# The first gate/up pair by seven products in three chunk pairs instead of two, and two input groups fetched two loads apart

## The reference

```python
    h = h + jnp.concatenate([oa, ob, oc, od], axis=-1) @ w_out[i]
    y = _rms(h, norm_ffn_g[i])
    h = h + (jax.nn.silu(y @ w_gate[i]) * (y @ w_up[i])) @ w_down[i]
    y = _rms(h, norm_ple_g[i])
```

## Time and profile before

| | |
|---|---|
| median of 3 runs (lowest to highest) | 1379.96 us (1379.74 to 1380.36) |
| the profiled execution: its time, its span | 1380.99 us, 1379.2 us |
| matmuls | 6175, busy 1371.7 us of the span |
| weight chunks split on VectorE, whole (L1391), from `w_raw` and from sums | 431 and 104 |
| DMA from HBM | 296.19 MB read, 27.31 MB written, 235 GB/s |

### The profile page before, as it was taken

One profiled execution on the slowest core, in us unless ns is written; L12 is line 12 of the kernel. 1 busy time (PEld: TensorE's weight loads), 2 busy tenths in 40 slices (PEclk: granted clock), 3 DMA queues, 4 the chain that ended last, 5 costly groups with the idle time before them and its releaser, 6 DMA issues.

```text
span 1379.2 us, 16905 instructions
## 1 busy us (share of the span) xinstructions
PE 1371.7 (99%) x6175; PEld 1123.2 (81%) x6175; DVE 1142.5 (83%) x1315; ACT 878.5 (64%) x1173; POOL 151.2 (11%) x127
## 2 busy tenths in 40 slices
PE   9999999999999999999999999999999999999998
PEld 7888888888888888788888888888888887777886
DVE  6589986688999988899999889976666769886897
ACT  7476755576777555677756576755566656675564
POOL 2000010011111000111100011100000144420000
PEclk9999999999999999999999999999999999999999
DMA  9766658887999788899987889999877878889675
GB/s 334 247 212 212 201 161 283 273 247 242 293 283 262 229 261 256 251 275 264 282 267 245 247 258 248 278 318 298 257 238 270 282 237 261 271 253 294 197 249 169
DMA packets 182859, 351.90 MB, mean 255 GB/s; under 512 B 13073, under 2 KB 37901, under 8 KB 182648
## 3 DMA queue, kind: packets, MB, share of 16 engines
q1 hardware_dynamic: 160408, 291.66, 64.4%
q0 software_dynamic: 9280, 33.97, 12.6%
q10 hardware_dynamic: 13088, 25.18, 6.1%
HBM read 296.19 MB, written 27.31 MB: 235 GB/s over the span
## 4 chain that ended last, share of the span: by engine, by line
PE 84%; DVE 2%; DMA 1%; issue 1%; ACT 0%; POOL 0%; ACTq 0%; DVEq 0%; POOLq 0%
PE acc L2340 13%; PE acc L2343 13%; PE acc L2342 13%; PE acc L2159 11%; PE acc L2161 11%; PE acc L2160 11%; PE sp L2340 2%; PE tp L2340 2%; PE tp L2343 2%; PE tp L2342 2%; PE sp L2343 2%; PE sp L2342 2%; DMA wide<-w_raw 1%; PE sp L2455 1%; PE tp L2471 1%; DVE w_lo L1391 1%
## 5 line engine op out<-in xcount | busy, mean ns | idle before, releaser
L963 ACT ACTIVATE w_hi<-w_raw 128x1024 fp32r<-128x1024 f32 x453 | 474.2, 1056 | 308.6 <-PE acc L2161 207.5
L1391 DVE TENSOR_TENSOR w_lo<-w_raw,w_hi 128x1024 fp32r<-128x1024 f32 x431 | 523.5, 1228 | 150.3 <-ACT w_hi L963 147.8
L2159 PE MATMUL acc<-w_lo,hh 128*128 128x512 f32 x528 | 207.7, 393 | 0.0
L2161 PE MATMUL acc<-w_hi,hl 128*128 128x512 f32 x528 | 205.6, 389 | 0.0
L2160 PE MATMUL acc<-w_hi,hh 128*128 128x512 f32 x528 | 205.6, 389 | 0.0
L2340 PE MATMUL acc<-w_lo,yh 128*128 128x512 f32 x452 | 176.0, 389 | 0.0
L2342 PE MATMUL acc<-w_hi,yh 128*128 128x512 f32 x452 | 175.9, 389 | 0.0
L2343 PE MATMUL acc<-w_hi,yl 128*128 128x512 f32 x452 | 175.8, 389 | 0.0
L963 ACT ACTIVATE w_hi<-wide 128x1024 fp32r<-128x1024 f32 x104 | 110.2, 1060 | 71.9 <-DVE wide L1405 35.7
L1391 DVE TENSOR_TENSOR w_lo<-wide,w_hi 128x1024 fp32r<-128x1024 f32 x104 | 126.8, 1223 | 13.7 <-ACT w_hi L963 13.4
L2159 PE MATMUL acc<-w_lo,yh 128*128 128x512 f32 x352 | 137.6, 391 | 0.3 <-DVE w_lo L1391 0.3
(11 more groups left out here) (332 smaller groups left out, 2179.4 us busy)
## 6 DMA issues: line engine op xcount, KB each, us to landing
w_raw<-in_w_gate SPq DMA_DIRECT2D x88, 512.0 KB, 5.8
w_raw<-in_w_up SPq DMA_DIRECT2D x88, 512.0 KB, 6.3
w_raw<-in_w_down SPq DMA_DIRECT2D x88, 512.0 KB, 6.3
w_raw<-in_w_in SPq DMA_DIRECT2D x64, 512.0 KB, 4.6
wide<-w_raw POOLq DMA_DIRECT2D x52, 512.0 KB, 6.0
w_raw<-in_swa_w_in ACTq DMA_DIRECT2D x48, 512.0 KB, 5.0
w_raw<-in_w_out SPq DMA_DIRECT2D x32, 512.0 KB, 5.9
w_raw<-in_w_ple_gate SPq DMA_DIRECT2D x32, 512.0 KB, 5.3
```

The lines of the kernel that those rows point to most:

```text
L963: act.activation(w_hi[:, v % SPL], src, ACT.Copy).then_inc(hi_ready, 1)
L1391: dve.tensor_tensor(w_lo[:, v % SPL], src, w_hi[:, v % SPL].bitcast(F32), ALU.subtract).then_inc(lo_ready, 1)
L2159: pe.matmul(dst, xh[:, f, tk], w_lo[:, v % SPL, k], start=(f == 0), stop=False)
L2161: last = pe.matmul(dst, xl[:, f, tk], w_hi[:, v % SPL, k], start=False, stop=(f == CK * end + CK - 1))
```

## The change

`FIRST_PLAN` gets a third pair of chunks by seven products (chunks 2 of gate and up), and a new order: it begins with the first two quads, and the plain chunk 3 of gate and up comes after the middle. It has 22 items instead of 20, from the same 16 loads. `FIRST_AT` moves the other work: the third input group is taken behind item 1 instead of 3, the residual addition behind item 2 instead of 1, turn and squares behind 3 instead of 2, the fourth group behind 14 instead of 10, `m1`, `mix`, `gate` and `silu` behind 18 to 21. In SyncE's queue the put of the third group stands behind load 1 and its fetch behind load 3 (both behind load 4 before), the put of the fourth behind load 7 and its fetch still behind load 9.

```diff
-FIRST_PLAN = plain(0, 2) + plain(1, 2) + plain(0, 3) + plain(1, 3) + quad("g", 0) + quad("g", 1) + quad("u", 0)
-FIRST_PLAN += plain(0, 4) + quad("t", 0) + quad("s", 0) + plain(1, 4) + quad("u", 1) + plain(0, 5) + quad("t", 1)
-FIRST_PLAN += quad("s", 1) + plain(0, 6, 7) + plain(1, 5, 6, 7)
-FIRST_AT = dict(pool_low=19, resid=1, turned=2, low2=3, request=3, low3=10, m1=13, mix=18, gate=19, silu=19,
-                copied={2: [0], 5: [1]}, summed={0: 6, 1: 11})
+FIRST_PLAN = quad("g", 0) + quad("g", 1) + quad("u", 0) + plain(0, 4) + plain(1, 4) + quad("t", 0) + quad("s", 0)
+FIRST_PLAN += quad("u", 1) + plain(0, 5) + quad("t", 1) + quad("s", 1) + plain(1, 5) + quad("g", 2) + quad("u", 2)
+FIRST_PLAN += plain(0, 3) + plain(1, 3) + quad("t", 2) + quad("s", 2) + plain(0, 6, 7) + plain(1, 6, 7)
+FIRST_AT = dict(pool_low=21, low2=1, resid=2, turned=3, request=4, low3=14, m1=18, mix=19, gate=20, silu=21,
+                copied={0: [0], 4: [1], 10: [2]}, summed={0: 4, 1: 7, 2: 14})
...
-                if i == 4:
-                    move(T_FFN + 2)
+                if i == 1:
+                    put(T_FFN + 2)
+                if i == 3:
+                    fetch(T_FFN + 2)
+                if i == 7:
+                    put(T_FFN + 3)
                 if i == 9:
-                    put(T_FFN + 3)
                     sp_.wait_ge(turned_lo, low_count(T_FFN + 2))
                     fetch(T_FFN + 3)
```

## The result

The changed kernel takes 1387.14 us (median of five runs, 1385.54 to 1389.36), the kernel before 1379.96 (1379.65 to 1380.36, five runs): a ratio of 1.0047, interval 1.0035 to 1.0058. It is slower, by about 6.5 us by the ratio. The forecast, 1384.0, had the sign and not the size: 4.0 us of 6.5. The median lies 0.5 above the end of the range, 1386.6; by the ratio the time is 1386.4, just inside it.

The account below looks back on a forecast made before the run. TensorE, busy 99% of the span, was taken to set the end, with the order of the queues in front of it deciding. Saving, front and end, -0.68 + 3.20 + 1.48 = +4.0 us, gave 1384.0 us, range 1381.6 to 1386.6.

Parts of the forecast that it names:

- The saving: TensorE in the first gate/up pair: 183 matmuls in place of 186 save 0.68 us.
- The front: First items of the block: TensorE waits for late w_lo at items 3, 4, t, s and 8, 3.20 us in all.
- The end of the block: Two plain items instead of three after the last gate item: the next block starts 0.82 us late.
- Inside the second pair: VectorE enters the second pair less far ahead, so TensorE waits 0.25 + 0.27 + 0.02 us more there.
- in the third: Third pair, where VectorE has no lead at one place: TensorE waits 0.12 us more.
- Puts, fetches, loads 8 and 9: SyncE's queue: the new order costs 0 to 1.1 us, the latter if loads 8 and 9 land late; taken as 0.
- The failed step: GpSimd's third add, issued near 309.2, takes about 5.8 us; sum due near 315.6, product wanted at 323: hidden, no cost.
- A: Rival: VectorE runs at least 2.1 us ahead before t, so only the 0.68 saving is left: 1379.3 us; 10%.
- B: Rival: VectorE is about 1 us further ahead at w_lo(4), half of the later waits is left: 1381.6 us; 8%.
- The highest-occupancy rule: Optimise the engine with the highest occupancy first, here TensorE; by it alone the change gives -0.68 us.
- C: Rival: the third input group lands 1.0 us late, or loads 8 and 9 cost 1.1, or both: 1385 to 1386.1; 15%.
- D: Rival: new gaps bring TensorE's clock from 2.4 to 1.2 GHz, 50 matmuls cost 11 us more: 1395; 2%.

Follow-up runs that it names:

- e9: e7 with ScalarE's third copy of tops ahead of item 12 instead of item 10; 1380.71 us, ratio 1.0002.
- e1: The changed kernel with the first sum of weights behind item 3 instead of item 4; 1387.69 us, ratio 1.0051.
- e3: The changed kernel with chunks 2 of gate and up as plain items, so two quads, 186 matmuls and no third add; 1384.95 us, ratio 1.0033.
- e8: e2 with a new end: three plain items behind the last gate item, gate chunk 6 ahead of the last sums; 1382.5 us, ratio 1.0015.
- e4: The kernel before with only SyncE's new order of puts and fetches; 1380.59 us, ratio 1.0002.
- e5: The changed kernel's new plan with SyncE's old order of puts and fetches; 1387.79 us, ratio 1.0056.
- e6: e2 with the first sum and the second copy of tops one item earlier; 1382.79 us, ratio 1.002.
- e7: The edits of e6 and e8 together, front and end; 1381.71 us, ratio 1.0009.
- e2: The changed kernel with loads 12 to 15 held until GpSimd's third add by DMA has landed; 1385.14 us, ratio 1.0035.

## Why the prediction was wrong in size

The sign, the places and the sizes of the waits at the front and at the end were right; one term, put at nothing, was not.

- **The saving.** 3 x 0.2267 = 0.68 us: right. The page has three matmuls fewer, and e9, in which the order costs next to nothing, comes out within 0.1% of the kernel before.
- **The front.** Forecast 0.14 + 0.69 + 0.35 + 1.59 + 0.43 = 3.20; measured 0.13, 0.58, 0.33, 1.57, 0.39 = 3.00, at the items named. Following three queues with the durations of the rows was good to 0.11 us in each term. That the chain from the first sum to t and s is its core is shown by e1 (the sum moved by one item, both waits gone), that the third quad has no part in it by e3.
- **The end of the block.** Forecast 0.82, measured 0.85; shown by e8, where one more item under the gate sum and silu removes it. Inside the second pair 0.34 instead of 0.54, in the third 0.11 instead of 0.12. Sum 1.30 for 1.48. In e8 the second pair's waits went with the end's, which bears out that they were its late start handed on.
- **Puts, fetches, loads 8 and 9.** Taken as 0 of a possible 1.1: right for the changed kernel (0.08 at the second quad's s), and e4 shows it for the queue by itself in the old plan. With the new plan the new queue does matter: e5, without it, waits at load 10. And the 0 held only for this front: with the front mended, load 9 is what ScalarE waits for, 3.96 us in e1, 2.19 in e6 and 3.10 in e7.
- **The failed step: "GpSimd's third add by DMA takes about 5.8 us [...] hidden".** The place (309.2) was right and the duration was not: 9.5 us instead of 5.8, and the sum that waits for it stalls VectorE's queue until 318.72, not 315.6. TensorE did not wait for the third quad's product, which the forecast had as its only reader, but for item 15, whose low part stands behind the sum in VectorE's order. It cost 1.74 us where 0 was given, and no bound was kept for it. The row that was used is a median over eight adds of 140 us; in the changed kernel's page the median of 53 adds is 6.2, while the one that mattered met five loads. e2 shows the cause: 6.1 us with three of the five held back. With 1.74 added, the forecast of 1384.0 becomes 1385.7; the ratio puts the kernel at 1.0047 x 1379.96 = 1386.4.
- **Sum.** By its own terms the profiled execution should have taken 1385.0 and took 1385.91: +1.74 for the add, -0.20 at the front, -0.18 at the end, +0.08 at the second quad give +1.44, and the stretch before the first pair was 0.45 shorter: 1386.0. The third pair starts at 379.63, forecast 379.0: the later pairs did not win the time back.
- **The rivals.** A (the saving stays) and B (half of it) would need VectorE 1 to 2 us earlier at item 4; its low part there ends at 298.39, 0.5 before the 298.91 of the forecast, and 0.45 of that is the earlier start of the whole stretch. Both are refuted. The highest-occupancy rule of the Trainium skill, "Perfetto Trace Analysis", section "Identifying the Most-Contended Engine", taken alone as the prediction took it, would have given 0.68 less; measured were 6.5 more. The same section does not take TensorE's matmul share as a measure of its headroom and looks at the share of its weight loads instead, which is 81% in the earlier trace rows, beside VectorE's 83%. C (transfers) had the right kind of event at two wrong transfers, and its 15% were too few for "some transfer of this block lands late", which happened in the profiled executions of five of the eight kernels with three quads (the changed one, e1, e5, e6, e7; in e1, e6 and e7 it is load 9, which C names). The range reached to 1386.6 only for the sake of C, whose two events cost 0.08 here. That the time by the ratio lies inside it is luck. D (the clock): not in the profiled run, but in e1 in full, at 2.8 us, a quarter of the 11 that it was priced at.

What stays open: the median of the changed kernel is 1.2 us above its profiled run. Its longest run (1389.36) has a mean clock of 0.999, and so have runs of e1; the two longest of e5 (1388.89 and 1390.0) have 0.998 and 0.999. That the wait of 1.74 grows in some executions until the clock falls, as in e1, would fit but was not traced, and 0.999 alone is no sign of it: the kernel before has it in a run of 1379.44 us.

## What to carry to other kernels

When work is added in front of an engine that is 99% busy, totals don't decide: write out the order of each queue item by item with the durations of the rows, and ask at each item how far ahead of the full engine its input stands. For a transfer on which an in-order queue will wait, don't take a median: list what other queues send in the microseconds around its issue, price it at the slowest row of its kind, and look at who stands behind the waiting instruction, since that one pays and not the transfer's reader. And when one wait is mended, look at once for the one that it was covering.

## What was unexpected of the hardware

- **One DMA, 6.1 to 9.5 us.** The add of 512 KB issued by GpSimd took 9.5 us from issue to landing with five loads of 512 KB sent by SyncE from 1.6 us before it to 0.4 us after, and 6.1 us at the same place with the last three of them held back. The Trainium skill says that another issuing engine gives no transfer a path of its own: in "DMA: Bandwidth & Descriptors", section "Issuing engines are not separate DMA queues", DMAs of all issuing engines end on the same 16 DMA engines and interleave. The two rows agree with it. A load of 512 KB on SyncE's queue also took 9.4 us in e1, among an add, a put, a fetch and other loads.
- **The clock after a pause.** In e1 a pause of 2.96 us of TensorE was followed by 6.2 us at a granted clock of 0.50, 1.2 GHz, which cost about as much as the pause itself. In e5 a pause of 2.6 us (its matmul at 320.25 above) was followed by matmuls at their usual distance (0.23 us, clock 1.00 over the run), and so was the one of 1.6 in the changed kernel. What decides it, these runs don't tell; two other runs of e5, not traced, have a mean clock of 0.998 and 0.999.
